# Moving six adaptive sums of the attention one step forward, from steps 3 and 9 to steps 2 and 8

## The chip, the cores and the metric

The kernel runs on one core of a Trainium2 chip. The metric is the device time of one execution in microseconds (us), as the median of the runs shown. One more execution was taken by the hardware profiler; the rows below come from it. TensorE is PE in the rows, its weight loads are PEld; VectorE is DVE, ScalarE is ACT, GpSimd is POOL, and SP is the engine whose queue issues the loads.

## The reference

Two blocks follow each other. The first has two layers of feed-forward, token mixer and feed-forward; the token mixer runs four kinds of attention over 512 tokens (`mla`, `diff`, and an `nsa` with selected and windowed keys and with compressed keys). The second is one adaptive block: nine vectors of 1024 are made from a condition and shift, scale and gate its layers. Cut to what matters here:

```python
for l in range(2):
    x = x + 0.5 * swiglu(rms_norm(x, ffn_norm_g[l, 0]), ...)
    x = x + token_mixer(rms_norm(x, mix_norm_g[l]), ...)   # the attentions
    x = x + 0.5 * swiglu(rms_norm(x, ffn_norm_g[l, 1]), ...)
...
m_l = split(silu(c) @ ada_w + ada_b, 9)       # ada_w is 1024 x 9216, fp32
m_c = split(silu(c_ctx) @ ada_w + ada_b, 9)
x = x + 0.5 * m_l[2] * swiglu_2(modulate(rms_norm_2(x, norm1_w), m_l[0], m_l[1]), ...)
```

## The kernel before

The products with `ada_w` don't depend on x. The kernel computes them inside the two attentions of the first block, 18 "adaptive sums" in each layer, every one over 1024 rows and 256 columns of `ada_w`, for both conditions at once.

**The attention** (`attention` on each engine; TensorE's begins at line 3394) is a software pipeline of 56 steps a layer: four passes, one for each tile of 128 queries, of 14 units with two attention maps each. `TILE_AT = (3, 0, 2, 1)` gives the order, so pass 0 scores 512 keys, pass 1 128 keys, pass 2 384 and pass 3 256. In step t TensorE does, in this order: the scores of unit t (lines 3413 and 3415; in step 1 also the compressed scores, line 3423, into bank 6), the turning of an adaptive result (line 3432) if the step before closed a group of sums, the transposes of the probabilities of unit t-3 (line 3447), the output matmuls of unit t-4 (lines 3483 and 3490), and an adaptive sum (line 3515) if the step is in the list `ADA_STEPS`. In the steps of the `diff` units (2 to 5 of a pass) only one map is turned, and output matmuls come once for two units: at the ends of steps 6 and 8 there are none. VectorE's step t has the negated maximum of unit t (`neg_max`, line 2455), a copy of the turned probabilities (2465), a reciprocal of unit t-1 (2470), the addition of an adaptive result into `mod` (2477) one step after its group closed, work of single steps (in step 2 four small instructions on the compressed scores, lines 2420 to 2427; in step 10 lines 2490 and 2491, which write `h_lo`), and at the end the copy of a closed group from PSUM into `diff_rows` (2498). ScalarE does the exponentials (1504), copies of turned probabilities (1494) and in step 10 a square and a copy (1518, 1519). POOL scales the probabilities once the reciprocal is there.

**The adaptive sums.** A sum at a step reads two halves of 512 KB from `ada_raw`, a ring with room for three halves: eight matmuls in the program, four for each half. A half is loaded by SP (line 900) as soon as the half that lay in its place is used up: load n waits until n-2 halves are used. Sums of one pass that stand in steps 4 to 9 form one group and share bank 7; the sum of step 2 or 3 is alone in bank 6, and starts only when VectorE has read the compressed scores out of it (line 3508). When a group is closed, VectorE copies it (2498), TensorE turns it in the next step (3432, waits for the copy) and VectorE adds it (2477).

**Who waits for the addition.** The output matmuls at step 4 write bank 6 and wait for the additions of all groups closed before (line 3479); at step 10 line 3465 makes the output matmuls that follow wait for the additions of all groups closed by then. At step 11 line 3469 waits for `h_lo` of line 2491.

Of the kernel before, what the change touches and what calls it, by code (L numbers as in the profile page):

```python
# [89 lines left out]
UN = len(UNIT_MAPS)  # L90
# [19 lines left out]
TILE_AT = (3, 0, 2, 1)  # L110


ADA_STEPS = [UN * i + at for i, steps in enumerate(((0, 2, 4, 6, 8, 13), (3, 6, 9), (3, 5, 7, 9, 13), (3, 5, 7, 9))) for at in steps]
ADA_AT = {t: n for n, t in enumerate(ADA_STEPS)}
ADA_GROUPS = []
for _n, _at in enumerate(ADA_STEPS):
    _bank = (_at // UN, 4 <= _at % UN < 10 or _at < UN - 4)
# [5 lines left out]
ADA_GROUP = {n: g for g, sums in enumerate(ADA_GROUPS) for n in sums}  # L123
ADA_ENDS = {ADA_STEPS[sums[-1]]: g for g, sums in enumerate(ADA_GROUPS)}
ADA_MOST = max(len(sums) for sums in ADA_GROUPS)
# [111 lines left out]
def build(nc, a, out):  # L237
    ctx = ExitStack()
    with ctx:
# [518 lines left out]
        def ada_bank(n):  # L758

            pos, step = divmod(ADA_STEPS[n], UN)  # L760
            return 6 if step > AT_SUMS or pos and step < AT_LAST else 7
# [3251 lines left out]
```

How the kernel before makes its waits and increments, by code:

```python
            def load_slot(turn, pos, dst, src):  # L774
                sp.wait_ge(lo_ready, turn * SLOTS + (pos + 1))
                sp.dma_start(dst, src).then_inc(slot_loaded[pos], 16)
# [58 lines left out]
                def load_params():  # L836
                    sp.wait_ge(*x_updated(layer, MIX_Y0))
                    for dst, src in (
                            (cmp_mask[:], a["c_cmp_mask"]),
                            (swap[:], a["c_swap"]),
# [10 lines left out]
                def load_aux(n):  # L852
                    v, c = n // AUX_V, n % AUX_V * AUX_PAIRS
                    sp.wait_ge(*aux_used(layer, n + 1 - AUX_RING))
                    sp.dma_start(aux[:, n % AUX_RING, :].rearrange("p (c h) -> p c h", c=AUX_PAIRS),
                                 a["nsa_cmp_w1"].rearrange("l v (c p) h -> (l v) p c h", p=P)[layer * 2 + v][:, c:c + AUX_PAIRS, :]
                                 ).then_inc(aux_loaded[n % AUX_RING].sem, 16)
# [35 lines left out]
                def load_ada(n):  # L894
                    if n == 0:
                        sp.wait_ge(*roped(layer, EVENTS - 5))
                    if n >= ADA_RING:
                        sp.wait_ge(*ada_used(layer, n + 1 - ADA_RING))
                    sp.dma_start(ada_raw[:, n % ADA_RING, :].rearrange("p (k n) -> p k n", k=ADA_K),
                                 ada_w[:, n % 2 * ADA_K:(n % 2 + 1) * ADA_K, bass.ds(layer * (ADA_SLOTS * P) + n // 2 * 2 * P, 2 * P)]
                                 ).then_inc(aux_loaded[n % ADA_RING].sem, 16)
```

## Time and profile before

| | us |
|---|---|
| median of 3 runs | 3546.88 |
| lowest and highest | 3545.88 and 3547.21 |
| the profiled execution | 3541.27 |
| its span | 3539.3 |
| TensorE busy in the span | 3464.1 |
| POOL, VectorE, ScalarE busy | 1550.2, 1663.5, 1476.7 |

The span runs from the first to the last instruction of the program; the profiled execution was 5.6 us shorter than the median. The attention of layer 0 runs from 540.0 to about 700 us of the span, that of layer 1 from about 1605 to about 1768. Pass 1 of layer 0 begins at 585.7, pass 2 at 617.0, pass 3 at 659.3. A "busy" matmul can contain short stalls, since ends are modelled; the number in square brackets at the end of a timeline row is the idle time of the engine before it, with the instruction that ended it.

### The profile page before, as it was taken

Reading aid. Unit: us, or ns where it says so; the run is one execution under the profiler, and the core shown is the slowest. Engines: PE = TensorE matmul, PEld = TensorE weight load, DVE = VectorE, ACT = ScalarE, POOL = GpSimd, SP = SyncE. Lnnn points to the kernel's source line nnn. Section 1 sums busy time; section 2 is a strip of 40 time slices with the busy share of each in tenths; the row PEclk is TensorE's granted clock in tenths of the full one; section 3 lists DMA queues with packets and bytes.
Section 4 is the critical chain, followed back from the end, with each engine's and each line's share of the span. In section 5 each row is a group of like instructions: output and inputs, shape, how many; then the busy total and the mean of one; then the engine's idle time right before and its main releaser. Section 6 shows DMA issues by size and latency. Waiting matters only on the chain.

```text
span 3539.3 us, 56010 instructions
## 1 busy us (share of the span) xinstructions
PE 3464.1 (98%) x21291; PEld 2903.6 (82%) x21291; DVE 1663.5 (47%) x2762; ACT 1476.7 (42%) x2450; POOL 1550.2 (44%) x1384
## 2 busy tenths in 40 slices
PE   8999999999999999999999999999999999999998
PEld 7999776689998999776589997888888785778887
DVE  8456634574658556644575656111112504651112
ACT  5344535553546344535554544212112335443223
POOL 4555545445545554545445544232323542034443
PEclk9999999999999999999999999999999999999999
DMA  4343444223433343444223333222222323023332
GB/s 125 106 113 85 105 131 126 90 77 103 118 87 93 100 115 85 108 126 133 90 72 107 107 90 96 66 60 65 59 61 58 90 59 101 19 61 100 96 95 65
DMA packets 569569, 322.57 MB, mean 91 GB/s; under 512 B 30282, under 2 KB 563376, under 8 KB 569008
## 3 DMA queue, kind: packets, MB, share of 16 engines
q1 hardware_dynamic: 569392, 320.22, 31.7%
q8 instruction: 110, 1.80, 0.2%
q14 instruction: 67, 0.55, 0.1%
HBM read 318.08 MB, written 2.10 MB: 90 GB/s over the span
## 4 chain that ended last, share of the span: by engine, by line
PE 65%; issue 22%; POOL 8%; DVE 3%; ACT 1%; POOLq 0%; ACTq 0%; DVEq 0%
PE psum L3100 21%; PE psum L2993 16%; PE psum L3207 12%; POOL w_lo L985 7%; PE psum L3413 2%; PE psum L3490 2%; PE psum L3447 1%; PE psum L3387 1%; PE psum L3134 1%; PE psum L3515 1%; PE psum L3137 1%; PE psum L3254 1%; PE psum L3532 1%; PE psum L3415 1%; POOL set_lo L1040 0%
## 5 line engine op out<-in xcount | busy, mean ns | idle before, releaser
L985 POOL TENSOR_TENSOR w_lo<-w_raw,w_hi 128x512 fp32r<-128x512 f32 x488 | 656.1, 1367 | 1109.2 <-ACT w_hi L1077 1109.2
L1077 ACT ACTIVATE w_hi<-w_raw 128x1024 fp32r<-128x1024 f32 x244 | 257.6, 1058 | 843.1 <-PE psum L2993 710.2
L2993 PE MATMUL psum<-h_hi,w_hi 128*128 128x512 f32 x1136 | 454.5, 400 | 1.5 <-POOL w_lo L985 1.5
L2993 PE MATMUL psum<-h_hi,w_lo 128*128 128x512 f32 x1136 | 447.2, 394 | 0.0
L2993 PE MATMUL psum<-h_lo,w_hi 128*128 128x512 f32 x1136 | 444.3, 391 | 0.0
L1040 POOL TENSOR_TENSOR set_lo<-w_raw,set_hi 128x512 fp32r<-128x512 f32 x224 | 292.5, 1333 | 223.3 <-ACT set_hi L1156 220.3
L3100 PE MATMUL psum<-t_hi,set_hi 128*128 128x256 f32 x1280 | 363.6, 284 | 9.9 <-ACT gated L1146 8.0
L3100 PE MATMUL psum<-t_lo,set_hi 128*128 128x256 f32 x1280 | 362.7, 283 | 0.0
L3100 PE MATMUL psum<-t_hi,set_lo 128*128 128x256 f32 x1280 | 362.7, 283 | 0.0
L3207 PE MATMUL psum<-a_hi,set_hi 128*128 128x512 f32 x704 | 277.0, 393 | 2.8 <-DVE a_lo L2142 2.8
L3207 PE MATMUL psum<-a_lo,set_hi 128*128 128x512 f32 x704 | 274.2, 389 | 0.0
L3100 PE MATMUL psum<-b_hi,set_hi 128*128 128x256 f32 x960 | 272.3, 284 | 1.8 <-DVE gated L2214 1.8
L3207 PE MATMUL psum<-a_hi,set_lo 128*128 128x512 f32 x704 | 274.0, 389 | 0.0
L3100 PE MATMUL psum<-b_lo,set_hi 128*128 128x256 f32 x960 | 271.9, 283 | 0.0
L3100 PE MATMUL psum<-b_hi,set_lo 128*128 128x256 f32 x960 | 271.8, 283 | 0.0
L2993 PEld LDWEIGHTS psum<-h_hi,w_hi 128*128 128x128 f32 x1136 | 213.3, 188 | 60.4 <-issue 10.9
L1022 POOL TENSOR_TENSOR set_lo<-w_raw,set_hi 128x512 fp32r<-128x512 f32 x160 | 212.6, 1349 | 113.6 <-ACT set_hi L1133 107.4
L1028 POOL TENSOR_TENSOR set_lo<-w_raw,set_hi 128x512 fp32r<-128x512 f32 x160 | 210.9, 1340 | 114.8 <-ACT set_hi L1136 114.8
L2108 DVE TENSOR_TENSOR gated<-silu_g,psum 128x512 f32<-128x512 f32 x66 | 37.6, 597 | 474.8 <-ACT silu_g L1201 474.8
L3100 PEld LDWEIGHTS psum<-t_hi,set_hi 128*128 128x128 f32 x1280 | 246.1, 192 | 11.8 <-POOL set_lo L1022 7.8
L2993 PEld LDWEIGHTS psum<-h_lo,w_hi 128*128 128x128 f32 x1136 | 213.3, 188 | 50.4 <-issue 4.3
L2993 PEld LDWEIGHTS psum<-h_hi,w_lo 128*128 128x128 f32 x1136 | 213.3, 188 | 46.0
(628 smaller groups left out, 8019.4 us busy)
## 6 DMA issues: line engine op xcount, KB each, us to landing
w_raw<-ffn_w SPq DMA_DIRECT2D x120, 512.0 KB, 3.8
w_raw<-ffn_w_gate SPq DMA_DIRECT2D x88, 512.0 KB, 4.1
w_raw<-ffn_w_up SPq DMA_DIRECT2D x88, 512.0 KB, 4.0
ada_raw<-ada_w SPq DMA_DIRECT2D x72, 512.0 KB, 4.7
w_raw<-ffn_w_down SPq DMA_DIRECT2D x64, 512.0 KB, 3.8
w_raw<-w_in SPq DMA_DIRECT2D x60, 512.0 KB, 3.9
w_raw<-ffn_w_down SPq DMA_DIRECT2D x32, 384.0 KB, 3.2
w_raw<-w_out SPq DMA_DIRECT2D x24, 512.0 KB, 3.6
```

The source lines that it names most:

```text
L985: last = nc.gpsimd.tensor_tensor(w_lo[:, i, at], w_raw[:, i, at], w_hi[:, i, at].bitcast(F32), ALU.subtract)
L1022: last = nc.gpsimd.tensor_tensor(lo[:, at], w_raw[:, 2 * r, at], hi[:, at].bitcast(F32), ALU.subtract)
L1028: last = nc.gpsimd.tensor_tensor(lo[:, to], w_raw[:, 2 * r + 1, at], hi[:, to].bitcast(F32), ALU.subtract)
L1040: last = nc.gpsimd.tensor_tensor(set_lo[i // 2][:, to], w_raw[:, i, at], set_hi[i // 2][:, to].bitcast(F32), ALU.subtract)
L1077: nc.scalar.activation(w_hi[:, pos, :], w_raw[:, pos, :], ACT.Copy).then_inc(hi_ready, 1)
L2108: last = nc.vector.tensor_tensor(gated[:, i, o:o + n], silu_g[:, i, o:o + n], up, ALU.mult)
L2993: last = nc.tensor.matmul(dst, w[:, pos, k * P:(k + 1) * P], rhs[g][r](k0 + k), start=k == 0 and m == 0, stop=k == nk - 1 and m == 2)
L3100: last = nc.tensor.matmul(dst, w[r][:, at], x[:, k, cols], start=not onto and k == 0 and m == 0, stop=k == HALF_K - 1 and m == 2, skip_gro ...
L3134: nc.tensor.matmul(bank[:, half * HALF_T:(half + 1) * HALF_T], w, (lo if m == 1 else hi)[:, k, :], start=k == m == half == 0, stop=False, ...
L3207: last = nc.tensor.matmul(psum[:, 6 + i % 2, :], w[i // 2][:, at], x[:, k, :], start=k == m == 0, stop=k == nf - 1 and m == 2)
L3413: nc.tensor.matmul(banks[m][:, 0:n], q(slice(tile * P, (tile + 1) * P)), k(n), start=True, stop=False)
L3490: last = nc.tensor.matmul(o_place(kind, h), v(b), probs_t[e % 2][:, x, b * P:(b + 1) * P], start=first and b == 0, stop=final and b == TIL ...
```

## The change

One line changes: the list of the steps at which sums stand. Pass 0 keeps (0, 2, 4, 6, 8, 13). In the passes 1, 2 and 3 the sum of step 3 moves to step 2, and the sum of step 9 moves to step 8. In passes 2 and 3 the sums of steps 7 and 8 then stand in adjacent steps. The groups, the banks, the number of sums and all loads stay the same. The order of instructions changes on TensorE and VectorE alone; SP, POOL and ScalarE have the same rows as before.

```diff
-ADA_STEPS = [UN * i + at for i, steps in enumerate(((0, 2, 4, 6, 8, 13), (3, 6, 9), (3, 5, 7, 9, 13), (3, 5, 7, 9))) for at in steps]
+ADA_STEPS = [UN * i + at for i, steps in enumerate(((0, 2, 4, 6, 8, 13), (2, 6, 8), (2, 5, 7, 8, 13), (2, 5, 7, 8))) for at in steps]
```

TensorE, pass 2 of layer 0, from the end of step 2 to the first output matmuls of step 4. L3515 is the sum, L3432 the turning, L3447 the transposes, L3490 output matmuls:

```order
 L3490 MATMUL psum<-probs_t_140,v_slc 64x128 x6
+L3515 MATMUL psum<-ada_raw,cond 32x256 x8
 L3413 MATMUL psum<-k_diff,q_diff 128x384 x2
 L3415 MATMUL psum<-causal_b,ident_b 128x128 x2
+L3432 MATMUL psum<-cond_sum,diff_rows 128x2 x2
 L3447 MATMUL psum<-ident,probs 128x128 x6
 L3490 MATMUL psum<-probs_t_138,v_win 64x128 x2
-L3515 MATMUL psum<-ada_raw,cond 32x256 x8
 L3413 MATMUL psum<-k_diff,q_diff 128x384 x2
 L3415 MATMUL psum<-causal_b,ident_b 128x128 x2
-L3432 MATMUL psum<-cond_sum,diff_rows 128x2 x2
 L3447 MATMUL psum<-ident,probs 128x128 x6
```

The sum now stands ahead of the scores of step 3, and the turning ahead of the transposes of step 3 instead of those of step 4.

VectorE at the same place, before: the four instructions on the compressed scores, then step 3 and the copy at its end.

```order
L2420 TENSOR_REDUCE cmp_stats<-cmp_p 128x8
L2422 RECIPROCAL cmp_stats<-cmp_stats 128x8
L2424 TENSOR_TENSOR cmp_stats<-cmp_stats,gates 128x8
L2427 TENSOR_SCALAR cmp_stats<-cmp_stats 128x8
L2455 TENSOR_REDUCE neg_max<-psum 128x2
L2465 COPY probs_t_140<-psum 128x384
L2470 RECIPROCAL scaled_inv<-exp_sum 128x2
L2498 COPY diff_rows<-psum 128x256
```

And now:

```order
L2422 RECIPROCAL cmp_stats<-cmp_stats 128x8
L2424 TENSOR_TENSOR cmp_stats<-cmp_stats,gates 128x8
L2427 TENSOR_SCALAR cmp_stats<-cmp_stats 128x8
L2498 COPY diff_rows<-psum 128x256
L2455 TENSOR_REDUCE neg_max<-psum 128x2
L2465 COPY probs_t_140<-psum 128x384
L2470 RECIPROCAL scaled_inv<-exp_sum 128x2
L2477 TENSOR_TENSOR mod<-psum,mod 128x2x2
```

The copy now stands right behind the compressed scores' four instructions and ahead of the `neg_max` of step 3; the addition ends step 3.

TensorE, pass 2, steps 7 to 10 in the changed kernel:

```order
L3490 MATMUL psum<-probs_t_140,v_diff 64x128 x6
L3515 MATMUL psum<-ada_raw,cond 32x256 x8
L3413 MATMUL psum<-k_slc,q_nsa 128x384 x2
L3415 MATMUL psum<-causal_b,ident_b 128x128 x2
L3447 MATMUL psum<-ident,probs 128x128 x3
L3515 MATMUL psum<-ada_raw,cond 32x256 x8
L3413 MATMUL psum<-k_win,q_nsa 128x384 x2
L3415 MATMUL psum<-causal_b,ident_b 128x128 x2
L3432 MATMUL psum<-cond_sum,diff_rows 128x6 x2
L3447 MATMUL psum<-ident,probs 128x128 x6
L3490 MATMUL psum<-probs_t_138,v_diff 64x128 x6
L3413 MATMUL psum<-k_slc,q_nsa 128x384 x2
```

The second L3515 stood behind the L3490 of step 9 before, and its L3432 behind the scores that are the last row but for their mask; between the two sums now lie the scores of one step and three transposes.

## Rows read from the trace of the kernel before

**Rows 1.** The page, chain that ended last, share of the span by engine

```profile
PE 65%; issue 22%; POOL 8%; DVE 3%; ACT 1%; POOLq 0%; ACTq 0%; DVEq 0%
```

**Rows 2.** Lines 2477 (who waited) and 3483 (its waits), whole trace: us, times

```profile
  PE psum L3490: 4.4, 6
...
  DVE probs_t L2465: 4.9, 6
```

**Rows 3.** Timeline, PE, pass 2 steps 3 and 4: start, us, line, xcount [idle before]

```profile
624.39 0.91 PE L3413 MATMUL psum<-k_diff,q_diff 32*128 32x384 f32 x4
...
629.19 0.61 PE L3432 MATMUL psum<-cond_sum,diff_rows 128*128 128x2 f32 x4 [0.57 <-DVE diff_rows L2498]
...
631.38 0.88 PE L3490 MATMUL psum<-probs_t,v_mla 128*64 128x128 f32 x12 [0.87 <-DVE mod L2477]
```

**Rows 4.** Timeline, DVE, pass 2 step 3

```profile
627.33 0.95 DVE L2455 TENSOR_REDUCE neg_max<-psum 128x2 f32<-128x768 f32 x1
...
628.73 0.40 DVE L2498 COPY diff_rows<-psum 128x256 f32<-128x256 f32 x1
```

**Rows 5.** Timeline, DVE and PE, pass 3 steps 3 and 4

```profile
670.50 0.69 DVE L2455 TENSOR_REDUCE neg_max<-psum 128x2 f32<-128x512 f32 x1
...
674.34 0.66 PE L3490 MATMUL psum<-probs_t,v_mla 128*64 128x128 f32 x8 [0.74 <-DVE mod L2477]
```

**Rows 6.** Timeline, PE, pass 2: scores of step 9, outputs of steps 10 and 11

```profile
642.18 0.92 PE L3413 MATMUL psum<-k_win,q_nsa 64*128 64x384 f32 x4
...
648.90 0.44 PE L3483 MATMUL psum<-cmp_pt,v_cmp 128*64 128x128 f32 x4 [0.95 <-DVE probs_t L2465]
...
651.65 0.88 PE L3490 MATMUL psum<-probs_t,v_win 128*64 128x128 f32 x12
```

**Rows 7.** Line 900, loads: pass 2, pass 3, pass 1 (landing alone), all 72

```profile
L900 SPq DMA_DIRECT2D ada_raw<-ada_w x1: 368/368/368, 640.5 to 640.5; - x1
DMA to landing us min/median/max: 3.8/3.8/3.8
...
L900 SPq DMA_DIRECT2D ada_raw<-ada_w x1: 368/368/368, 681.7 to 681.7; - x1
DMA to landing us min/median/max: 3.4/3.4/3.4
...
DMA to landing us min/median/max: 4.0/4.0/4.0
...
DMA to landing us min/median/max: 3.4/4.7/7.6
```

**Rows 8.** Timeline, PE, pass 3: scores of step 9, outputs of step 10

```profile
683.12 0.70 PE L3413 MATMUL psum<-k_win,q_nsa 64*128 64x256 f32 x4
...
688.66 0.44 PE L3483 MATMUL psum<-cmp_pt,v_cmp 128*64 128x128 f32 x4 [0.81 <-DVE probs_t L2465]
```

**Rows 9.** Timeline, PE, pass 1: outputs of step 4, scores of 7 and 9, outputs of 10

```profile
600.32 0.44 PE L3490 MATMUL psum<-probs_t,v_mla 128*64 128x128 f32 x4 [0.61 <-DVE mod L2477]
...
605.25 0.49 PE L3413 MATMUL psum<-k_win,q_nsa 64*128 64x128 f32 x4
...
607.31 0.49 PE L3413 MATMUL psum<-k_win,q_nsa 64*128 64x128 f32 x4
...
611.72 0.44 PE L3483 MATMUL psum<-cmp_pt,v_cmp 128*64 128x128 f32 x4 [0.67 <-DVE probs_t L2465]
```

**Rows 10.** Timeline, DVE, pass 2 step 10: first and last of the chain to `h_lo`

```profile
646.88 0.96 DVE L2455 TENSOR_REDUCE neg_max<-psum 128x2 f32<-128x768 f32 x1 [0.61 <-PE psum L3415]
...
650.20 0.41 DVE L2491 TENSOR_TENSOR h_lo<-psum,h_hi 128x256 fp32r<-128x256 f32 x1
```

**Rows 11.** Stretches: us, busy (x) of PE, PEld, DVE, ACT, POOL; then PEclk, DMA, GB/s

```profile
601.39:604.79 3.40, 3.40 (x27) 2.01 (x29) 1.90 (x7) 1.89 (x9) 2.89 (x7) 0.50 0.36 126
...
649.18:652.57 3.39, 3.39 (x42) 2.33 (x39) 2.23 (x5) 1.62 (x7) 0.84 (x2) 1.00 0.28 98
...
1697.07:1703.88 6.81, 6.81 (x46) 3.47 (x43) 1.72 (x3) 2.03 (x6) 4.53 (x7) 0.50 0.03 3
```

## The prediction

> **What bounds the kernel now.** I read the page first, then the waits of single lines, then the timeline of the attention of layer 0 engine by engine, then the landing times of the loads. The chain that ended last is to 65% TensorE's own work and to 22% its issue; VectorE, ScalarE and POOL have 12% together [rows 1]. So what the change touches is worth the time in which TensorE stands still or runs slowly in the two attentions, and little else: a transfer or a copy that TensorE doesn't wait for is free. Two waits hang on the adaptive sums. At step 4 the first output matmuls (line 3490) wait until VectorE has added the last result into `mod` (line 2477): 4.4 us in 6 places, three to a layer. At step 10 the output matmuls that start with line 3483 stand 4.9 us in 6 places [rows 2]. The trace puts these down to `probs_t`, but that copy is of an earlier step; line 3465 makes TensorE wait there for the same addition, which VectorE does just after a `probs_t` copy of step 10. So the prize has a ceiling: 9.3 us of 3547, or 0.26%.
>
> **Step 3 to step 2.** Eight matmuls of a sum, 1.0 us, move one step forward in three passes of each layer; no instruction is added or dropped on any engine, and SP, POOL and ScalarE keep their order. What moves with them is VectorE's copy (0.40 us) and the addition.
> Pass 1: VectorE is idle there, TensorE is what everybody waits for. The gap of 0.61 us before line 3490 at step 4 [rows 9] goes: -0.6.
> Pass 2: VectorE is late here. Its four small instructions on the compressed scores end only when `neg_max` starts, at 627.33; now the copy comes there first, until 627.73, and `neg_max` of step 3 starts 0.4 later [rows 4]. TensorE leaves step 2 at 624.39 [rows 3], then needs 1.0 for the sum and 1.1 for the scores of step 3, so from 626.5 it stands before line 3432 until about 627.75: 1.25 us. Before, it stood 0.57 and 0.87 us [rows 3]. The gap has moved one step and keeps most of its size: -0.2. Bounds: -1.4 if VectorE catches up, +0.7 if POOL, which gets its factor some 0.7 later, is late for the transposes two steps on.
> Pass 3: likewise. VectorE is free at 670.50, the copy ends at 670.92, TensorE would be there some 0.4 earlier; the 0.74 before line 3490 goes [rows 5]. -0.3.
>
> **Step 9 to step 8.** Here the loads decide. A sum reads two halves of 512 KB; three halves fit in `ada_raw`. The second half of the sum of step 8 goes where the first half of the sum before lay, so SP can issue it only when the first four matmuls of that one are done. Before, a whole step with its output matmuls and a second step lay between; now in passes 2 and 3 it is the very next step, and a short one: a `diff` unit of one slot, without output matmuls.
> Pass 2: SP issued that load at 640.5 and it landed 3.8 us later, at 644.3 [rows 7]. The sum of step 8 would start where the scores of step 9 started, at 642.18 [rows 6]; its first half takes 0.5, so TensorE stands from 642.7 to 644.3: +1.6.
> Pass 3: issued at 681.7, landed 3.4 later, 685.1 [rows 7]. The sum would start at 683.12 [rows 8], its first half ends 683.6: +1.5.
> Pass 1: the two sums are two steps apart, steps 6 and 8, but steps of 128 keys are short. From the sum's end, where step 7 starts at 605.25, to the scores of step 9 at 607.31 are 2.06 us [rows 9]; with 1.0 for the sum and 0.5 for the first half of the next the second half is wanted 3.55 after the sum's start. It is there after 0.7 (first half, and SP's start) plus 4.0 [rows 7]: +1.15.
> These stand on the least and the usual landings: over all 72 loads of the trace landings go from 3.4 to 7.6 [rows 7]. From 3.4 everywhere (-1.0 to a layer) to 5.0 (+4.0 to a layer) are the bounds; I take the rows of the places themselves.
> The Trainium skill, "DMA: Bandwidth & Descriptors", section "Anatomy of one DMA", gives about 2.0 us plus bytes over 436 GB/s, an estimate of 3.2 us for 512 KB, for the path that GpSimd issues. That is under every landing in this trace [rows 7]; by it the three waits of a layer would be 1.6 us shorter, and the sum below would be 3.2 us less. I don't use it.
>
> **Step 10.** The addition now stands in step 9, so the gaps of 0.67 [rows 9], 0.95 [rows 6] and 0.81 [rows 8] us go. But what follows was hidden behind them. At step 11 line 3490 also waits for `h_lo` (line 2491), the end of a chain through `neg_max`, ScalarE's exponentials, square and copy, and two VectorE instructions: in pass 2 from 646.88 to 650.61 [rows 10], 1.0 before TensorE asked at 651.65 [rows 6]. In the changed kernel the scores of step 10 stand 2.0 later (1.6 for the wait, 0.4 for line 3432, which now comes ahead of them), so `h_lo` is ready near 652.6, while TensorE would be there 0.6 later than before, at 652.3. +0.3 in pass 2; +0.5 in pass 3, where the slack is less by my reading of the same chain; and in pass 1, where TensorE waited for `h_lo` already, I book only 0.05 of the 0.67.
>
> **The clock.** The granted clock of TensorE was half (1.2 instead of 2.4 GHz) in 3.4 us of pass 1, right after its gap of 0.61, and in 6.8 us of pass 2 of layer 1 [rows 11], after the two gaps that pass 2 has in layer 0 too [rows 3]; pass 1 of layer 1 has the same stretch as layer 0. Of the 12 places with gaps of 0.6 to 1.4 us three were followed by such a stretch. A stretch costs up to half its length. In pass 1 the gap goes and so, I think, does the stretch: of 1.7 us I take 1.1, as VectorE and POOL don't get faster. The six new waits, at 3 in 12, give 1.5 stretches of 1.7: +2.6 over both layers; the long one of layer 1 (3.4 at most) goes with 2 chances in 3: -2.3. Together +0.3.
> The Trainium skill, "TensorE: Matmul & The Clock Gate", Part 1, holds that the throttled state is the default and activity lifts it, which speaks against new waits of TensorE. The trace agrees in 3 places of 12; what each wait would cost if it held everywhere is the third case.
>
> **Sum.** Pass 1: -0.6 - 1.1 + 1.15 - 0.05 = -0.6. Pass 2: -0.2 + 1.6 - 0.95 + 0.3 = +0.75. Pass 3: -0.3 + 1.5 - 0.8 + 0.5 = +0.9. A layer +1.05, both +2.1, with the clock +2.4. The profiled execution took 3541.27 us (span 3539.3), 5.6 under the median of the runs; I put the difference on the median: 3546.9 + 2.4 = 3549.3.
>
> **The ways it could go.**
> 1. As summed: the gaps of the additions are traded for waits for loads. 3549.3, between 3543.5 and 3553. 62%.
> 2. The loads are hidden after all and every gap goes: 3546.9 - 9.3 = 3537.6, and less if half-clock stretches go with them. It needs landings of 2.2 us, and the shortest is 3.4 [rows 7]. 4%.
> 3. Slower: each wait for a load drops the clock. Six stretches of 1.7 make +10.2, with the 2.1 of the passes +12.3: 3559.2. It decides from the third stretch on (2.1 + 5.1 = 7.2). For it: gaps of 0.61 were enough in pass 1. Against: 0.95 in pass 2 was not, the clock stayed at 1.00 behind it [rows 11]. 13%.
> 4. The copy ahead of `neg_max` at step 2 makes POOL late, and TensorE waits 0.7 more in passes 2 and 3: +2.8, 3552.1. For it: `neg_max` does move by 0.4. Against: what POOL scales there is wanted three steps after its scores, so it has most of two steps in hand. 8%.
> 5. All three half-clock stretches go and none comes: 2.4 - 2.6 - 1.1 = -1.3, 3545.6. 10%.
> 6. The change doesn't do what it says: the sum of step 2 is held by the compressed scores (line 3508) and so starts no earlier than at step 3. Then step 4 stays as it was in all passes, and 0.6, 1.1, 0.2 and 0.3 a layer are not gained: +4.4 more, 3553.7. Against: VectorE is through with the whole of that block, four instructions on, at 627.33 even in pass 2, where it is late [rows 4], and has taken the scores out of their bank long before. 3%.
>
> What this kernel's runs can tell from no change is about 0.2%, 7 us. Faster by that needs case 2: 4%. Slower needs case 3 or long landings in case 1: 13%. Within it 83%. The range leaves out case 2 and the upper part of case 3: 3542.5 to 3556.
>
> **What would show it.** In the changed trace TensorE waits for `ada_raw` at line 3515 in all three passes of both layers, 1 to 1.7 us each, some 8.5 us in all; nobody waits for line 2477 any more, and line 3483 no longer stands at step 10; instead line 3432 waits for the copy at step 3, 1.25 in pass 2 and 0.4 in pass 3, and line 3490 for `h_lo` at step 11. I am wrong if the second halves land before TensorE wants them, if the first gaps vanish in passes 2 and 3, or if the granted clock falls after most of the waits.

## The result, and the profile after

The changed kernel took 3556.49 us (median of 13 runs, 3547.05 to 3565.89); the kernel before, on the same chip, 3545.10 (13 runs, 3540.07 to 3548.82). The ratio is 1.0037, 95% interval [1.0028, 1.0047]. A second measurement, with new runs of the kernel before beside it, gave 3555.14 against 3540.07 and again 1.0037 [1.0023, 1.0051]. So the change makes the kernel slower by 0.37%, 13 us by the ratio (10 to 17 by its interval), where I had forecast 2.4 us, which these runs can't tell from no change. The measured median lies half a microsecond outside the range; by the ratio (3546.9 x 1.0037 = 3560.0) it is case 3, which I gave 13%, that named the closest time.

The profiled execution took 3560.46 us (span 3558.5). Its chain of work that ended last has less of TensorE than before and more of issue and POOL, and a share of DMA that was not there [rows 1]:

```profile
PE 59%; issue 25%; POOL 10%; DVE 2%; ACT 1%; DMA 1%; POOLq 0%; ACTq 0%; DVEq 0%; SPq 0%
```

The waits of TensorE in the attention of layer 0 (line and releaser: us in total, times, longest) answer [rows 2]:

```profile
PE psum L3515 <- DMA ada_raw<-ada_w: 4.9, 5, 1.6
PE psum L3490 <- issue: 2.0, 3, 1.1
PE psum L3432 <- DVE diff_rows L2498: 1.7, 2, 1.3
...
PE psum L3515 <- issue: 0.4, 1, 0.4
```

The two old waits are gone: nobody waits for the addition at line 2477 at step 4, and line 3483 no longer stands at step 10. In their place stand waits for loads (line 3515), for the copy of the rows (3432) and for `h_lo` (3490). Here they are in the timeline of TensorE, in passes 1, 2 and 3 of layer 0 (start, us, line, and the idle time before it in brackets); they answer [rows 3, 5, 6, 8, 9]:

```profile
609.45 0.64 PE L3515 MATMUL psum<-ada_raw,cond 128*32 128x256 f32 x8 [1.00 <-DMA ada_raw<-ada_w]
615.27 0.44 PE L3490 MATMUL psum<-probs_t,v_win 128*64 128x128 f32 x4 [1.07 <-issue]
...
629.71 0.61 PE L3432 MATMUL psum<-cond_sum,diff_rows 128*128 128x2 f32 x4 [1.29 <-DVE diff_rows L2498]
...
650.76 0.64 PE L3515 MATMUL psum<-ada_raw,cond 128*32 128x256 f32 x8 [1.64 <-DMA ada_raw<-ada_w]
...
659.15 0.88 PE L3490 MATMUL psum<-probs_t,v_win 128*64 128x128 f32 x12 [0.29 <-issue]
...
678.48 0.61 PE L3432 MATMUL psum<-cond_sum,diff_rows 128*128 128x2 f32 x4 [0.37 <-DVE diff_rows L2498]
684.34 1.07 PE L3515 MATMUL psum<-ada_raw,cond 128*32 128x256 f32 x16 [0.41 <-issue]
...
689.86 0.64 PE L3515 MATMUL psum<-ada_raw,cond 128*32 128x256 f32 x8 [0.44 <-DMA ada_raw<-ada_w]
693.09 0.64 PE L3515 MATMUL psum<-ada_raw,cond 128*32 128x256 f32 x8 [0.95 <-DMA ada_raw<-ada_w]
700.14 0.66 PE L3490 MATMUL psum<-probs_t,v_win 128*64 128x128 f32 x8 [0.68 <-issue]
```

Most of these are where the forecast had put them, and of its size; not forecast were the 0.41 and the 0.44 at line 3515 in pass 3, and 1.07 at step 11 of pass 1 is more than was booked. What was missed most is seen in the stretches. First the passes of the kernel before: 1, 2 and 3 of layer 0, then 2 of layer 1 (from:to, us, busy us of PE, PEld, DVE, ACT, POOL, then the mean granted clock of TensorE, DMA share, GB/s):

```profile
585.68:617.02 31.34, 29.80 (x317) 20.76 (x313) 15.90 (x57) 15.65 (x70) 15.11 (x32) 0.95 0.45 136
617.02:659.32 42.30, 39.53 (x377) 23.62 (x375) 24.00 (x58) 24.13 (x77) 22.92 (x35) 1.00 0.33 101
659.32:700.34 41.02, 39.16 (x412) 26.33 (x408) 21.99 (x62) 22.06 (x77) 20.51 (x36) 1.00 0.30 91
...
1682.17:1727.58 45.41, 42.63 (x377) 25.02 (x375) 24.01 (x58) 24.02 (x77) 22.91 (x35) 0.92 0.30 93
```

The same view of the changed kernel: passes 1 to 3 of layer 0, then 1 and 2 of layer 1:

```profile
587.85:618.91 31.06, 28.76 (x317) 20.06 (x313) 15.91 (x57) 15.62 (x70) 15.09 (x32) 1.00 0.43 137
618.91:666.81 47.90, 44.30 (x376) 25.99 (x375) 24.21 (x58) 24.35 (x77) 22.93 (x35) 0.89 0.29 89
666.81:709.72 42.91, 39.75 (x412) 26.23 (x408) 21.79 (x62) 22.27 (x77) 20.52 (x36) 1.00 0.28 87
1661.76:1694.53 32.77, 31.57 (x316) 21.58 (x312) 16.12 (x57) 15.65 (x70) 15.09 (x32) 0.90 0.42 130
1694.53:1742.41 47.88, 44.32 (x376) 26.53 (x374) 24.22 (x58) 24.46 (x77) 22.92 (x35) 0.89 0.28 89
```

And the stretches in these passes in which the granted clock was 0.50 (1.2 GHz), which answer [rows 11]:

```profile
630.95:641.19 10.24, 10.24 (x62) 5.97 (x65) 4.00 (x9) 5.14 (x16) 6.86 (x10) 0.50 0.06 19
1685.67:1692.49 6.82, 6.82 (x41) 4.05 (x40) 2.45 (x11) 3.29 (x16) 2.63 (x6) 0.50 0.26 77
1706.15:1712.97 6.82, 6.82 (x35) 4.19 (x35) 2.88 (x7) 3.73 (x11) 3.60 (x5) 0.50 0.16 53
1726.63:1730.03 3.40, 3.40 (x23) 2.74 (x24) 1.56 (x4) 1.62 (x5) 0.87 (x2) 0.50 0.59 183
```

Pass 2 grew from 42.30 to 47.90, and pass 3, at full clock, from 41.02 to 42.91. The attentions of both layers together grew by 13.0 us. The half-clock time in them doubled, from 13.7 us (3.4, 3.4 and 6.8) to 27.3. The longest stretch, 10.24 us, begins 1.2 us after the stand of 1.29 at line 3432, the next long one of pass 2 0.8 after that of layer 1; the other two begin 2.3 and 1.8 after waits for loads. The rest of the program was 6.2 us longer in this execution, with 43 us at half clock there against 30. Those 6.2 us are not the change's: outside the four passes of both layers the profiles of e5 to e8 below, which all have both moves, took 3215.3 to 3216.2 us, and the kernel before 3215.5. Nor are the 13.0 us of the attentions the change's cost as such: the profiled execution of the kernel before (3541.27) lies 3.8 us under the 3545.10 of its runs, that of the changed kernel 4.0 over its own median.

### The profile page after: what moved, and what is told of

The parts are those of the page before. It is cut to its first block, busy times and chain, and to the rows that moved or that the text cites. A ratio compares the mean times of both kernels' runs of the same rounds, so it can differ in the third digit from the quotient of the medians.

```text
span 3558.5 us, 56010 instructions
## 1 busy us (share of the span) xinstructions
PE 3477.9 (98%) x21291; PEld 2913.3 (82%) x21291; DVE 1663.5 (47%) x2762; ACT 1480.8 (42%) x2450; POOL 1550.8 (44%) x1384
## 4 chain that ended last, share of the span: by engine, by line
PE 59%; issue 25%; POOL 10%; DVE 2%; ACT 1%; DMA 1%; POOLq 0%; ACTq 0%; DVEq 0%; SPq 0%
PE psum L3100 21%; PE psum L2993 14%; PE psum L3207 11%; POOL w_lo L985 9%; PE psum L3413 2%; PE psum L3490 2%; PE psum L3447 1%; POOL set_lo L1040 1%; PE psum L3134 1%; PE psum L3137 1%; DMA ada_raw<-ada_w 1%; PE psum L3515 1%; PE psum L3532 1%; PE psum L3387 1%; PE psum L3415 0%
```

## The experiments

Three theories. C: a good part of the loss is the clock that falls behind the new stands. L: it is the stands themselves, the waits for loads above all. V: it is VectorE, whose copy of the rows now goes ahead of `neg_max` at step 2 while TensorE stands at line 3432. Each kernel ran beside the kernel before on the same chip; three sets of four, four and three kernels, and one alone. All half-clock counts are of the profiled execution.

**Each half of the change alone.** e1_step2 moves only 3 to 2, e2_step8 only 9 to 8 (of `ADA_STEPS` the table alone, against the kernel before):

```diff
-((0, 2, 4, 6, 8, 13), (3, 6, 9), (3, 5, 7, 9, 13), (3, 5, 7, 9))
+((0, 2, 4, 6, 8, 13), (2, 6, 9), (2, 5, 7, 9, 13), (2, 5, 7, 9))
...
-((0, 2, 4, 6, 8, 13), (3, 6, 9), (3, 5, 7, 9, 13), (3, 5, 7, 9))
+((0, 2, 4, 6, 8, 13), (3, 6, 8), (3, 5, 7, 8, 13), (3, 5, 7, 8))
```

> Only the sums of step 3 move to step 2; those of step 9 stay. Theory C (the clock): what the change costs over the forecast comes from stretches at half clock, above all behind the new wait of line 3432 at step 3 of pass 2, so half of the loss is here already: 1 to 6 us slower than before, with 7 to 10 us at half clock in pass 2 of both layers, and none in pass 1. Theory L (the loads): the waits for ada_raw at step 8 and what they delay cost it all, so this part alone is 2 to 5 us faster than before. Theory V (VectorE's copy ahead of neg_max slows the softmax chain): 4 us or more slower, with longer waits for probabilities in passes 2 and 3 and a full clock.

> Only the sums of step 9 move to step 8; those of step 3 stay. Theory L: 11 to 14 us slower than before, the whole loss. Theory C: 4 to 8 us slower: about 8.5 us of waits for ada_raw against 4.9 us of gaps at step 10, some of them kept waiting at step 11, and one or two stretches at half clock. Theory V: 3 to 5 us slower.

Measured: 3 to 2 alone 3541.70 us, ratio 0.9999 [0.9989, 1.0010]; 9 to 8 alone 3552.55, ratio 1.0034 [1.0019, 1.0048]. So the whole net loss comes with 9 to 8, and 3 to 2 gives nothing on the whole. For 9 to 8, theory L's 11 to 14 us came (12 by the ratio, 7 to 17 by its interval), C's 4 to 8 and V's 3 to 5 did not. For 3 to 2 (0 us, by the interval 4 faster to 4 slower) none of the three times came: V's 4 us or more slower is all but excluded, C's half of the loss is not there, and L's 2 to 5 faster is only within the interval. The profile of e1 had full clock in all six passes, and so shows what the move of 3 to 2 does without the clock (passes 1, 2, 3 of layer 0):

```profile
584.29:614.11 29.82, 28.69 (x316) 20.18 (x312) 15.92 (x57) 15.43 (x70) 15.19 (x32) 1.00 0.45 143
614.11:656.18 42.07, 39.46 (x377) 23.59 (x375) 24.01 (x58) 24.24 (x77) 23.00 (x35) 1.00 0.32 101
656.18:697.45 41.27, 39.39 (x413) 26.42 (x409) 21.86 (x62) 21.95 (x77) 20.62 (x36) 1.00 0.29 90
```

Against the passes before: -1.52 (with the half-clock stretch that pass 1 had), -0.23, +0.25. So C's 7 to 10 us at half clock in pass 2 were not there in this execution, though TensorE stood 1.28 before line 3432 in both layers.

**The turning behind the outputs.** In e4_turn_behind (on e1) and e5_after_behind (on the changed kernel) the turning of the sum of step 2, line 3432, moves in step 3 from ahead of the transposes to behind the output matmuls, so TensorE has work while VectorE is late:

```diff
-                    if t - 1 in ADA_ENDS:
...
+                    if t - 1 in ADA_ENDS and step != 3:
+                        turn_sums()
...
+                    if t - 1 in ADA_ENDS and step == 3:
+                        turn_sums()
                     if t in ADA_AT:
```

> As e1_step2, but the turning of the sum of step 2 (line 3432) stands at the end of step 3, behind the transposes and the output matmuls, so that TensorE doesn't wait there for VectorE's copy while it has work. Theory C: no stretch at half clock in passes 1 and 2, 4 to 9 us faster than before. Theory V: the copy still stands ahead of neg_max, so the time is within 1.5 us of e1_step2. Theory L says nothing against a gain of 3 to 5 us here.

> The changed kernel with the turning of the sum of step 2 at the end of step 3. Theory C: 5 to 9 us faster than the changed kernel, so 3 to 7 us slower than before: the waits for loads stay, the stretch of pass 2 behind step 3 goes. Theory L: as the changed kernel within 3 us, 10 to 13 us slower than before. Theory V: as the changed kernel.

Measured: e4 3533.27, ratio 0.9973 [0.9964, 0.9983], that is 0.0026 or 9 us under e1 by the ratios; e5 3546.26, ratio 1.0016 [1.0004, 1.0028], 7.4 us under the changed kernel. C's times came (e4's by half a microsecond over its 4 to 9). L had e5 within 3 us of the changed kernel, and missed. V had e4 within 1.5 us of e1 and e5 at the time of the changed kernel, and falls: the copy still stands ahead of `neg_max` in both. The stand of 1.28 in pass 2 became one of 0.25 (e4, TensorE, same place; line 3432 is 3408 there):

```profile
627.72 0.61 PE L3408 MATMUL psum<-cond_sum,diff_rows 128*128 128x2 f32 x4 [0.25 <-DVE diff_rows L2498]
```

At full clock this is worth 1.1 in pass 2 (40.97 and 40.99 against 42.07) and 0.5 in pass 3 of layer 1 (40.77 against 41.27), 3.2 in both layers if pass 3 of layer 0, which in e4 waited 0.76 for a load, is counted like that of layer 1:

```profile
616.93:657.90 40.97, 39.40 (x376) 23.62 (x374) 23.92 (x58) 24.31 (x77) 22.99 (x35) 1.00 0.34 104
...
1721.03:1761.80 40.77, 39.25 (x412) 26.43 (x408) 21.87 (x62) 22.05 (x77) 20.61 (x36) 1.00 0.29 92
```

The rest of the 7 to 9 is then not the stand itself. The mean granted clock over all runs rose with it: 0.9942 in e1, 0.9959 in e4. At two levels, 2 x (1 - clock) x time is the time at half clock: 41 us a run in e1, 29 in e4. Half of the 12 between them would be the 6 us that are left.

**Filling the wait for the load.** In e6_fill8 TensorE does 4, 6 and 4 matmuls that nobody reads where it would stand for the second half at step 8; e7_fill8_behind adds the same to e5. The waiting time stays, the idleness goes.

```diff
                         for half in range(2):
+                            if half and i and step == 8:
+                                pe.wait_ge(*probs_t_act(layer, event_of(t - 4) + 1))
+                                for _ in range((0, 4, 6, 4)[i]):
+                                    nc.tensor.matmul(psum[:, 4, 0:P], ident[:], ones[:], start=True, stop=True)
                             pe.wait_ge(*ada_loaded(layer, 2 * n + half))
```

> The changed kernel with filler: at step 8 of the three later query tiles, between the first and the second half of the adaptive sum, TensorE first waits for the same event that the outputs behind the sum wait for, then does 4, 6 and 4 extra matmuls of 128x128 (identity times ones, into a PSUM bank that nobody reads) in passes 1, 2 and 3, and only then waits for the second half of the load. The extra matmuls fill most of the 1 to 1.7 us in which TensorE stood there. Theory C (what the moved sum of step 9 to 8 loses is mostly the clock that falls behind the stand): the half-clock stretches behind step 8 go, about 15 us of half-clock time over the run with them, and the time is 5 to 7 us under the changed kernel: 3548 to 3551 on a chip on which that takes 3555. Theory L (it is the stand itself): the time is that of the changed kernel, 3554 to 3558, since TensorE waits for the load as long as before, only busy.

> The same filler, added to the kernel with both moves and the turning of the sum of step 2 behind the outputs of step 3 (its time without filler: 3546.3, with 3543.2 of the kernel before beside it). Theory C: the filler takes away the clock's share that is left, -4 to -5: 3541 to 3543. Theory L: as without filler, 3545 to 3548.

In pass 2 of layer 0 of e6 the filler (line 3516) ends as the load lands, and the second half follows without a gap:

```profile
643.38 0.64 PE L3519 MATMUL psum<-ada_raw,cond 128*32 128x256 f32 x8
643.95 1.60 PE L3516 MATMUL psum<-ones,ident 128*128 128x128 f32 x12
645.62 0.64 PE L3519 MATMUL psum<-ada_raw,cond 128*32 128x256 f32 x8
```

Measured: e6 3550.31, ratio 1.0022 [1.0013, 1.0031]; e7 3543.41, ratio 1.0000 [0.9992, 1.0009]. By the ratios that is 5.3 us under the changed kernel and 5.7 under e5, for work added and no wait shortened. In each pair the two intervals still overlap a little; that both pairs agree is what carries the 5 to 6 us. C's numbers came, L's did not (the upper end of e7's C is missed by 0.4). The mean granted clock of e6's runs is 0.9935, that of the kernel before beside it 0.9934. So at equal clock 0.0022, some 8 us, of the 13 are left, and some 5 were clock behind the waits for loads. The passes of e6 in layer 1, at full clock:

```profile
1660.03:1691.10 31.07, 29.77 (x324) 21.02 (x320) 15.89 (x57) 15.55 (x70) 15.14 (x32) 1.00 0.44 137
1691.10:1734.38 43.28, 41.20 (x389) 24.91 (x387) 24.01 (x58) 24.49 (x77) 22.94 (x35) 1.00 0.31 98
```

So the change's pass 2 without the clock is 43.28; the 47.9 of the changed kernel carry 4.6 us of clock.

**Smaller loads.** In e8_small_loads the second halves of the sums of step 8 in passes 1 to 3 are loaded by 32 of 256 columns; e11_small_behind does the same on e5. Those sums are not the reference's.

```diff
+                    cols = P // 4 if n % 2 and ADA_STEPS[n // 2] > UN and ADA_STEPS[n // 2] % UN == 8 else 2 * P
...
-                                 ada_w[:, n % 2 * ADA_K:(n % 2 + 1) * ADA_K, bass.ds(layer * (ADA_SLOTS * P) + n // 2 * 2 * P, 2 * P)]
+                                 ada_w[:, n % 2 * ADA_K:(n % 2 + 1) * ADA_K, bass.ds(layer * (ADA_SLOTS * P) + n // 2 * 2 * P, cols)]
```

> The changed kernel, but the second half of the weights of each sum that stands in a step 8 of the three later query tiles is loaded by 32 of its 256 columns only (64 KB instead of 512 KB; the other columns hold what an earlier load left there, so those adaptive sums are not the reference's). The transfer is then short enough to land before TensorE wants it. Theory L: the waits at line 3515 shrink from 1 to 1.7 us to under 0.4, the gaps of the additions stay away, and the time falls by 8 to 12 us under the changed kernel, to that of the kernel with the first move alone or below: 3538 to 3546 (0.997 to 1.001 of the kernel before). Theory C gives the same, since with the wait the half-clock stretches behind it go too. What would speak against both: a time within 3 us of the changed kernel; then the loss of 9 to 8 is neither the load nor the clock behind it, but the crowding of two sums in steps 7 and 8.

> Both moves, the turning of the sum of step 2 behind the outputs of step 3, and the second halves of the sums of step 8 of the three later query tiles loaded by 32 of 256 columns only (those adaptive sums are not the reference's). Both kinds of new stand are gone then. Theory C with the forecast's own gains (gaps of the additions gone: 0.3 to 0.9 each): passes of 29.8, 40.9 and 41.4 and few half-clock stretches, 3531 to 3535 on a chip on which the kernel before takes 3544 (0.9963 to 0.9975), about the same as the first move with the turning behind alone (0.9973). Rival: crowding of two sums in steps 7 and 8 costs by itself, 3538 to 3542.

The small loads of passes 1 to 3 of layer 0 landed after 2.4 us in the median, the large ones of the same stretch after 4.2 (issue, count, KB each, us to landing):

```profile
ada_raw<-ada_w SPq DMA_DIRECT2D x16, 512.0 KB, 4.2
ada_raw<-ada_w SPq DMA_DIRECT2D x3, 64.0 KB, 2.4
```

Measured: e8 3540.51, ratio 0.9999 [0.9988, 1.0010]; of the waits for loads in passes 1 to 3 only 0.39 and 0.16 us in pass 3 are left, and the loss of 9 to 8 is gone whole. Both theories had that, since the clock behind a wait goes with the wait; what it excludes is the crowding. The small loads also take 1.3 MB a layer off the DMA engines; no run shows whether that alone is worth anything, and the filler, which leaves the loads whole, is free of it. e11 3533.12, ratio 0.9975 [0.9967, 0.9984], with full clock in all six passes; passes 1 to 3 of layer 0:

```profile
585.65:615.48 29.83, 28.54 (x317) 20.20 (x313) 15.93 (x57) 15.66 (x70) 15.18 (x32) 1.00 0.41 127
615.48:655.80 40.32, 39.40 (x376) 23.62 (x374) 23.82 (x58) 24.57 (x77) 23.00 (x35) 1.00 0.31 94
655.80:696.73 40.93, 39.44 (x413) 26.37 (x409) 21.79 (x62) 22.31 (x77) 20.63 (x36) 1.00 0.26 80
```

This is what the change would have given with these loads in time and line 3432 behind the outputs. That two sums stand in adjacent steps costs nothing by itself. Taking the gaps of step 10 away is worth little beside that: e11 is no faster than e4 (0.9975 and 0.9973); in it TensorE stands 2.0 us a layer for `h_lo` at step 11, where e4 stands 2.4 at step 10.

**Pass 1 alone.** e3_pass1 moves only the sum of pass 1 from 3 to 2:

```diff
-((0, 2, 4, 6, 8, 13), (3, 6, 9), (3, 5, 7, 9, 13), (3, 5, 7, 9))
+((0, 2, 4, 6, 8, 13), (2, 6, 9), (3, 5, 7, 9, 13), (3, 5, 7, 9))
```

> Only one sum of a layer is moved: that of pass 1 from step 3 to step 2; passes 2 and 3 and all sums of step 9 stay as before. In pass 1 the copy of the rows comes in time, so line 3432 waits for nothing there. Theory C: the gain of pass 1 (1.5 us a layer with both moves of 3 to 2, the half-clock stretch behind its gap included) comes out whole, since no new stand is bought with it: 3 to 4 under the kernel before, ratio 0.9989 to 0.9992; the move of all three (0.9999) then loses its gain at the stands of passes 2 and 3 and the clock behind them. Rival: the gain of pass 1 was an accident of the profiled execution and the ratio is 0.9997 to 1.0003.

Measured: 3542.36, ratio 0.9998 [0.9988, 1.0008]; theory C's 0.9989 to 0.9992 is not met, though the interval still reaches its end. Pass 1 did come to 29.83 in both layers, but in pass 2, which was not changed, the clock fell in both layers, behind the old gap of 0.57 and inside that of 0.87, where in the kernel before it fell in one layer, behind both. The passes 2 of both layers and the stretch of layer 0:

```profile
614.27:659.45 45.18, 42.42 (x376) 25.21 (x375) 24.00 (x58) 24.06 (x77) 23.01 (x35) 0.92 0.29 94
...
1682.36:1727.68 45.32, 42.55 (x376) 25.27 (x375) 23.99 (x58) 24.04 (x77) 23.00 (x35) 0.92 0.29 94
...
628.16:634.98 6.82, 6.35 (x41) 3.86 (x45) 2.05 (x6) 3.03 (x10) 4.89 (x8) 0.50 0.13 47
```

So one profile's half-clock stretch is not a fixed property of a place, and a gain of 3 us cannot be separated from that in these runs.

**A better version.** e9_add_early is e4 with VectorE's addition (line 2477) ahead of its copy of the turned probabilities (2465), except at step 3. e10_pass0 is e9 with pass 0's sums in other steps, to take away the wait for a load that pass 0 always had.

```diff
+                    if t - 1 in ADA_ENDS and step != 3:
...
+                        dve.wait_ge(*ada_turned(layer, group + 1))
...
-                    if t - 1 in ADA_ENDS:
+                    if t - 1 in ADA_ENDS and step == 3:
...
-((0, 2, 4, 6, 8, 13), (2, 6, 9)
+((0, 3, 5, 7, 9, 13), (2, 6, 9)
```

> The first move alone (3 to 2), with the turning of the sum of step 2 behind the outputs of step 3 (that took 0.9973 of the kernel before), and VectorE's addition of the turned sums ahead of its probs copy in the step in which it stands, except at step 3. So the second half of the sum that follows an addition closely (step 10, behind the sum of step 9) should find it done sooner. Theory: the stands of 0.67, 0.95 and 0.8 us at step 10 of passes 1, 2 and 3 go, 2.4 a layer, 0 to -4 in all after what the later copy costs: 0.9962 to 0.9973 of the kernel before. Rival: VectorE's probs copy is wanted as early as the addition is, comes 0.3 to 0.4 us later in about nine steps a layer, and TensorE or POOL waits for that instead: 0 to +5, 0.9973 to 0.9987.

> The best version so far (first move, turning behind the outputs, VectorE's addition early: 0.9970) with the sums of pass 0 in steps 0, 3, 5, 7, 9, 13 instead of 0, 2, 4, 6, 8, 13. In pass 0 TensorE stands 1.06 to 1.4 us for the second half of the sum of step 2, and in two profiled executions of such kernels the clock was halved for 6.8 us right behind it (passes of 48.7 to 48.9 instead of 45.7). Theory C: with a step more the load has landed, the stand and the half-clock stretch behind it go, -1.2 and up to -1.5 more a layer where the stand is: 1 to 4 under that version, 0.9959 to 0.9968. Rival: the additions behind steps 3 and 9 bring gaps of 0.6 to 0.9 into pass 0 as they did into passes 1 to 3 before: 0 to +3, 0.9970 to 0.9979.

Measured: e9 3532.50, ratio 0.9970 [0.9960, 0.9980], the fastest of all, though its interval overlaps that of e4; the gap at step 10 of pass 2 fell from 0.94 to 0.18, and pass 2 from 40.97 to 40.21. This also bears out that the gaps of step 10 were waits for the addition, as the forecast had it, and not for the `probs_t` copy that the trace names: the copy came later here, and the gap went. e10 3535.81, ratio 0.9978 [0.9969, 0.9987]: the rival's time came. The wait for the load is gone from pass 0, but TensorE stands for ScalarE's exponentials and VectorE's copy instead (the rows name these, not the additions that the rival had in mind), and pass 0 took 46.80 at full clock in place of 45.67. TensorE's stands in pass 0 of layer 0:

```profile
548.00 1.13 PE L3430 MATMUL psum<-k_diff,q_diff 32*128 32x512 f32 x4 [0.63 <-ACT probs L1504]
553.61 0.66 PE L3457 MATMUL psum<-ident,probs 128*128 128x128 f32 x4 [0.67 <-DVE probs_t L2472]
```

And the stretch of that pass:

```profile
540.07:586.87 46.80, 44.84 (x407) 25.60 (x407) 26.72 (x49) 26.80 (x70) 27.30 (x33) 1.00 0.41 127
```

**The changed kernel again**, for a second profile:

> The changed kernel itself, once more, for a second profile: which of its half-clock stretches in the attention stand at the same places. Theory C: behind the 1.3 us for which line 3432 waits in pass 2, and behind the wait for the second half at step 8, the clock falls again at most of these places (in the first profile 27 us of half-clock time in the attention, against 13.7 before); in attention 15 us or more. Rival: the stretches of the first profile were its own accident; under 14 us in attention here. The ratio: 1.003 to 1.0045 by both, since it was measured so before.

Measured: 3555.14, ratio 1.0037 [1.0023, 1.0051]. The half-clock stretches in the attentions:

```profile
626.91:633.74 6.83, 6.83 (x36) 4.34 (x36) 2.82 (x8) 3.72 (x11) 3.54 (x5) 0.50 0.16 57
647.39:654.21 6.82, 6.82 (x37) 4.75 (x38) 2.61 (x5) 2.25 (x7) 1.31 (x2) 0.50 0.29 94
1623.60:1633.83 10.23, 10.23 (x50) 6.00 (x46) 4.93 (x10) 4.68 (x13) 4.45 (x6) 0.50 0.33 101
1688.45:1691.85 3.40, 3.40 (x23) 2.29 (x24) 1.41 (x6) 2.09 (x11) 1.77 (x4) 0.50 0.46 142
1708.93:1712.33 3.40, 3.40 (x24) 2.59 (x23) 1.63 (x4) 2.38 (x8) 2.84 (x5) 0.50 0.03 5
sum 30.68, PE 30.68 PEld 19.97 DVE 13.40 ACT 15.12 POOL 13.91; mean PE 6.14 PEld 3.99 DVE 2.68 ACT 3.02 POOL 2.78
```

30.7 us, with the first and the last again behind the stand of 1.28 at line 3432 (0.7 and 2.4 us), in both layers; the second and the fourth begin 1.7 and 2.5 behind waits for loads, and one is in pass 0, behind a wait of 1.58. The mean granted clock of its runs was 0.9920, that of the kernel before beside it 0.9947: 57 and 38 us at half clock. A stretch at half clock costs at most half its length (pass 2 of the changed kernel: 4.6 for 10.24), so at most 9.5 of the 15 us between the medians are clock.

## Why the prediction was wrong, step by step

**What held.** The reading of what bounds the kernel, the order of the loads, and nearly every wait. Load waits at step 8: 1.15, 1.6 and 1.5 forecast for passes 1 to 3; 1.00, 1.64 and 0.95 measured in layer 0 (pass 3 with another 0.44 at step 7), 0.97, 1.59 and 1.56 in layer 1. Line 3432: 1.25 and 0.4 forecast, 1.29 and 0.37 measured. `h_lo` at step 11 of passes 2 and 3: 0.3 and 0.5 forecast, 0.29 and 0.68 measured. The landings didn't change (3.5 to 7.0 us with a median of 4.7, against [rows 7]). VectorE's copy goes ahead of `neg_max`, as read from [rows 4]:

```profile
629.23 0.42 DVE L2498 COPY diff_rows<-psum 128x256 f32<-128x256 f32 x1
629.57 0.95 DVE L2455 TENSOR_REDUCE neg_max<-psum 128x2 f32<-128x768 f32 x1
```

**What was mis-sized in the passes.** At full clock passes 1 to 3 come to 31.06, 43.28 and 42.91, against 31.34, 42.30 and 41.02 before: -0.3, +1.0, +1.9, or +2.6 a layer where the sum had +1.05, so +5.2 in both where I had +2.1. (The 31.34 before holds 3.4 us at half clock, in both layers; the sum had booked 1.1 for that.)
Step 9 to 8 (the passes just named less those of e1): +1.2, +1.2 and +1.6, 4.1 a layer, where the terms had 1.1, 0.95 and 1.2. In pass 1 I let `h_lo` take back 0.62 of the 0.67 won at step 10; it took 1.07, and the load wait was 0.15 shorter than forecast. In pass 3 0.2 of the miss is `h_lo` (0.68 for 0.5); for the other 0.25 I found no row.
Step 3 to 2: passes 1 and 2 were right (-1.7 and -0.2 forecast, -1.52 and -0.23 in e1, though in pass 1 0.23 of the 0.61 comes back at line 3454, where TensorE waits for POOL), pass 3 was not: -0.3 forecast, +0.25 measured. The 0.74 before line 3490 went, but 0.37 came back at line 3432, which was forecast, and 0.41 at the sum of step 5, which was not. That sum waits (line 3511) for VectorE's `h_lo` of line 2443 (683.54 to 684.23; TensorE goes on at 684.34):

```profile
683.54 0.69 DVE L2443 TENSOR_TENSOR h_lo<-psum,h_hi 128x512 fp32r<-128x512 f32 x1 [1.18 <-ACT h_hi L1479]
```

I had looked one step beyond the removed gap for what is late next, not two.

**The step that failed: the clock.** It was booked at +0.3; the forecast had itself named "the granted clock falls after most of the waits" as what would make it wrong. The two parts of that term went differently.
For the loads, "at 3 in 12" was about right: in the four profiles with waits for loads of 0.95 us and more at step 8 (the changed kernel twice, e2 and e5), 7 of 23 were followed by half clock, 1.1 to 2.5 us behind the wait. But the stretches were 5.4 us long on average (three of 3.4, four of 6.8), not 3.4. With the idleness filled (e6, e7) there was none behind the 12 such places, and 5 to 6 us came back, where I had booked 2.6. (At 7 in 23 and 5.4 us, six waits give 9.9 us at half clock, which is 4.9 at most.)
For pass 2, "the long one of layer 1 goes with 2 chances in 3: -2.3" did not come. I had written that the gap "has moved one step and keeps most of its size", and yet counted its clock as gone. Two gaps of 0.57 and 0.87 became one of 1.28, and behind this the clock fell in 4 of 4 places of the changed kernel, 6.8 us on average, and in 7 of 10 over all profiles that have it, 4.1 us a place. Around the old pair of gaps it fell in 4 of 6 places (the kernel before, e2 and e3), 6.8 us each time, 4.6 a place. So the one stand is not shown to be worse than the two gaps were; it kept their clock. What it costs is seen where the turning went behind the outputs: none in 12 places (e4, e5, e7, e9, e10, e11), and the time fell by 7 to 9 us, of which the stands account for 3.
Together: the passes give 5.2 where I had 2.1, and the clock some 5 behind the loads and about nothing in pass 2 where I had 0.3. That is 10.5 of the 13, and within the interval of 10 to 17. At equal mean clock e6 leaves 8, and the 5.2 come near that when the 1.1 that were booked for the half clock of the old pass 1 are taken out in both layers (7.4). How much of the 13 is clock is known no better than that: some 5 by e6, at most 9.5 by the mean clocks.
The Trainium skill, "TensorE: Matmul & The Clock Gate", Part 1 ("HAM oscillation — how this bites in real kernels" and "A second HAM failure mode: psum-queue depth-cycling"), tells of a kernel whose every wait for a load, of some 3 to 5 us, leaves the work behind it at half clock, and of another in which frequent small idle times between groups of matmuls do. Here it was 7 of 23 for waits for loads of 0.95 to 1.94 us, and 7 of 10 for the 1.28 us at line 3432, so neither each time nor never; the sentence I had cited from that Part spoke against the change, and the price I set on it was too small.

**The other cases.** Case 2 can't be had with whole loads, but e11, whose small loads landed in 2.1 us in the median, once line 3432 was out of the way too, took 0.9975 of the kernel before, where case 2 had 3537.6 of 3546.9, which is 0.9974; that this agrees so closely is luck, since TensorE still stood 2.0 us a layer for `h_lo` and the half-clock stretches of the passes were gone as well. Case 3, "each load wait drops the clock", named nearly the right time by luck: three in ten of the load waits did, which cost some 5 us and not 10.2, and the passes lost 5.2 and not 2.1. Case 4 had the right copy, but POOL was not late for it; TensorE was the one that stood, at line 3432. Case 5 was opposite to what happened, and case 6 fell, since step 4 has no gap any more.

What stays open: why the clock fell at one place in one execution and not in the next.

## What to carry to other kernels

A wait that only moves keeps its price, and the clock behind it belongs to that: the stand of 1.28 kept what the gaps of 0.57 and 0.87 had cost. Work that waits for a late engine goes behind independent work of the same step (line 3432 behind the outputs: 7 to 9 us, in both kernels), and a load that must come earlier has to be released earlier; moving its user does not move it. When a gap is taken away, follow the chain until the next two waits, not the next one.

## What the runs showed of the hardware

The same kernel on the same chip differed by 8 to 20 us between executions, and its time followed the mean granted clock: a straight line through the runs of a kernel rises by 0.2 to 0.5 us for each us at half clock, in all 13 kernels (the clock of a run is on record to 0.001, which is 7 us at half clock, so these slopes are rough). Half-clock stretches of 3.4, 6.8 and 10.2 us came behind stands of 0.6 to 1.9 us among small matmuls, in some executions of a place and not in others. In pass 0, whose wait for a load was there before the change, they came behind stands of 1.23, 1.42, 1.58 and 1.59 us, and not behind those of 1.26 and 1.35 nor behind the other 20, of 0.78 to 1.13. Matmuls whose result nobody reads, put into such stands at step 8, made the kernel 5 to 6 us faster.
